# Nine closing operand splits of a two-block transformer kernel, moved on VectorE behind the weight split that followed them

## The reference, cut to what matters

```
u = rmsnorm(h, gain)          # h * rsqrt(mean(h*h)) * gain
h = h + mixer(u) @ w_out      # attention, gated delta rule, gated linear attention
u = rmsnorm(h, gain)
h = h + act(u @ w_up) @ w_down
```

## Time and profile before

| | us |
|---|---|
| median of 3 runs | 1652.29 |
| lowest, highest | 1652.26, 1653.44 |
| the profiled execution | 1653.44 |
| its span (first to last instruction) | 1651.6 |
| TensorE matmuls busy | 1575.7 (95%) |
| VectorE busy | 1119.3 (68%) |
| ScalarE busy | 792.4 (48%) |
| GpSimd busy | 185.2 (11%) |

### The profile page before, as it was taken

How to read it: one execution, slowest core, us unless ns; L and a number is a source line. 1 busy time by engine, 2 the same in 40 slices (tenths; PEclk the granted TensorE clock), 3 DMA queues, 4 the chain that set the end, 5 groups by cost and what they waited for, 6 DMA issues and landing times.

```text
span 1651.6 us, 31485 instructions
## 1 busy us (share of the span) xinstructions
PE 1575.7 (95%) x12628; PEld 1516.1 (92%) x12628; DVE 1119.3 (68%) x2014; ACT 792.4 (48%) x1360; POOL 185.2 (11%) x200
## 2 busy tenths in 40 slices
PE   6988899999998899999999899999989999999997
PEld 5875898999998699999899899999989899999997
DVE  5884654767775767777777766666677566666666
ACT  4537234533453454444655465544455556554443
POOL 2680411100012120000200012000020002010000
PEclk9998799999999999999999999999999999999999
DMA  6411001454454125455443343555534444254652
GB/s 217 154 52 52 1 1 52 154 190 167 169 188 150 65 103 187 170 203 175 165 165 118 143 155 103 180 178 204 174 139 173 153 154 166 90 190 168 205 179 77
DMA packets 125813, 236.55 MB, mean 143 GB/s; under 512 B 2615, under 2 KB 50026, under 8 KB 125690
## 3 DMA queue, kind: packets, MB, share of 16 engines
q1 hardware_dynamic: 124393, 230.29, 40.2%
q0 software_dynamic: 1296, 4.53, 0.9%
HBM read 233.76 MB, written 1.05 MB: 142 GB/s over the span
## 4 chain that ended last, share of the span: by engine, by line
PE 85%; DVE 9%; ACT 2%; issue 2%; DMA 1%; POOL 0%; SPq 0%; DVEq 0%; ACTq 0%; POOLq 0%
PE ps L613 48%; PE ps L660 6%; PE ps L659 6%; PE ps L658 6%; PE ps L621 5%; DVE w_lo L2212 3%; PE ps L803 2%; PE ps L764 1%; PE ps L987 1%; PE ps L709 1%; PE ps L969 1%; PE ps L744 1%; DVE mx L2558 1%; DVE hidden L2263 1%; ACT w_hi L1582 1%
## 5 line engine op out<-in xcount | busy, mean ns | idle before, releaser
L1582 ACT ACTIVATE w_hi<-raw 128x1024 fp32r<-128x1024 f32 x440 | 460.9, 1051 | 294.1 <-PE ps L660 137.9
L2212 DVE TENSOR_TENSOR w_lo<-raw,w_hi 128x1024 fp32r<-128x1024 f32 x440 | 544.8, 1239 | 8.1 <-ACT w_hi L1582 8.0
L613 PE MATMUL ps<-u_hi,w_hi 128*128 128x256 f32 (+1 forms) x1480 | 430.1, 291 | 11.9 <-DVE w_lo L2212 4.7
L613 PE MATMUL ps<-u_hi,w_lo 128*128 128x256 f32 (+1 forms) x1480 | 423.6, 286 | 0.0
L613 PE MATMUL ps<-u_lo,w_hi 128*128 128x256 f32 (+1 forms) x1480 | 423.2, 286 | 0.0
L613 PEld LDWEIGHTS ps<-u_hi,w_hi 128*128 128x128 f32 x1480 | 283.6, 192 | 17.3 <-issue 7.1
L613 PEld LDWEIGHTS ps<-u_hi,w_lo 128*128 128x128 f32 x1480 | 283.5, 192 | 0.0
L613 PEld LDWEIGHTS ps<-u_lo,w_hi 128*128 128x128 f32 x1480 | 282.6, 191 | 0.6
L613 PE MATMUL ps<-a_hi,w_hi 128*128 128x256 f32 (+1 forms) x864 | 246.4, 285 | 4.1 <-DVE a_lo L2232 2.0
L613 PE MATMUL ps<-a_lo,w_hi 128*128 128x256 f32 (+1 forms) x864 | 243.8, 282 | 0.0
L613 PE MATMUL ps<-a_hi,w_lo 128*128 128x256 f32 (+1 forms) x864 | 243.6, 282 | 0.0
(11 more groups left out here) (416 smaller groups left out, 2300.5 us busy)
## 6 DMA issues: line engine op xcount, KB each, us to landing
raw<-in_w_ff_dram SPq DMA_DIRECT2D x32, 2048.0 KB, 8.5
raw<-in_ffn_w_gu_dram SPq DMA_DIRECT2D x44, 1024.0 KB, 6.7
raw<-in_ffn_w_down_dram SPq DMA_DIRECT2D x10, 2048.0 KB, 7.9
raw<-in_xa_w_kv_dram SPq DMA_DIRECT2D x8, 2048.0 KB, 9.0
raw<-in_od_w_in_dram SPq DMA_DIRECT2D x6, 2048.0 KB, 8.1
raw<-in_w_in_ab_dram SPq DMA_DIRECT2D x5, 2048.0 KB, 7.9
raw<-in_ev_w_in_dram SPq DMA_DIRECT2D x5, 2048.0 KB, 7.9
raw<-in_xa_w_q_dram SPq DMA_DIRECT2D x4, 2048.0 KB, 7.8
```

The costliest lines, as they stand in the source:

```text
L613: mm = pe.matmul(bank[:, 0:n], wx[:, q, k * P:(k + 1) * P], x[ux][:, k, ts], start=k == 0 and i == 0, stop=k == KD - 1 and i == 2)
L1582: act.activation(quarter(w_hi, b, q), raw_quarter(b, q), ACT.Copy).then_inc(high_split, 1)
L2212: dve.tensor_tensor(quarter(w_lo, b, q), raw_quarter(b, q), quarter(w_hi, b, q).bitcast(F32), ALU.subtract)\
```

## The change

In `residual` and in `down`, the low part of the last chunk (k = 7) was issued right after that of chunk 6. It is now issued after the loop, that is behind the `split_low` of the next product's quarter 2, which came after it before. No instruction is added or removed, and only VectorE's queue changes.

```diff
@@ residual
                     if 4 * i + t >= 1:
                         finish_low(4 * i + t - 1, norm, ts)
-                    if 4 * i + t == KD - 1:
-                        finish_low(KD - 1, norm, ts)
                 stream(name, evac)
+                finish_low(KD - 1, norm, ts)
@@ down
                     if norm is not None and k >= 1:
                         finish_low(k - 1, norm, ts)
-                    if norm is not None and k == KD - 1:
-                        finish_low(k, norm, ts)
                     if k % 2 == 1:
                         split_low(b + 1, k // 2 - 1, g)
+                if norm is not None:
+                    finish_low(KD - 1, norm, ts)
```

## The result

| | before | after |
|---|---|---|
| median, us | 1652.55 (7 runs, 1651.36 to 1656.15) | 1671.59 (7 runs, 1659.86 to 1674.21) |
| ratio | | 1.0093, interval 1.0070 to 1.0115 |
| profiled execution: span, mean clock | 1651.6 us, 0.981 | 1661.9 us, 0.981 |

The change makes the kernel slower, as forecast, but by more than the range of the prediction held: its 1663.0 was the highest time allowed. The two profiled spans, which have the same mean clock, differ by 10.3 us; the medians of seven differ by 19.0. So there are two questions: what the move costs, and what stands between 10 and 19. An execution is one run of the whole kernel on the chip; executions of one and the same kernel differ here by 12 us and more.

What follows compares the result with a forecast made beforehand. The prediction took TensorE, 85% of the chain, as the bound. Its stalls, 3.80 + 0.66 + 3.42 + 0.8 = 8.7 us, on the median 1652.29 gave 1661.0, range 1656.0 to 1663.0.

Steps and rivals of the forecast that it cites:

- What moves, and who is late: At the nine seams: the split wins time, low 7 loses it, and TensorE waits for the later low 7.
- The earlier split: At the seams: writing quarter 2's weight split earlier is worth 0, being 2.9 us early already at c_out.
- the faster rival: TensorE waits for quarter 2 of the weights, so the earlier split pays 1.2 us nine times: 1641.5; chance 0.03.
- At a projection seam: Five seams of 256 tokens: TensorE stands 0.76 us for low 7 where it did not before, together 3.80 us.
- at ab_out: Seam ab_out to mlp0, 272 tokens: TensorE waits 0.66 us for the later low 7.
- At ev_in: Seam mlp1 to ev_in: TensorE already waits for low 7, which comes 1.71 us later in full.
- at od_in: Seam swiglu0 to od_in: same pattern as mlp1 to ev_in, 1.71 us again; together 3.42 us.
- at c_kv: Seam mlp0 to c_kv: the memory rows' load is issued later, costing 0.8 us; bounds 0.0 and 1.7.
- Low part ahead of the addition: At the seams: low 7 goes ahead of GpSimd's waiting addition; sum 5.1 us, 1657.4; chance 0.15.
- Full blocking behind a split: At eight seams: low 7 ends 0.48 us behind the addition, not 0.29; sum 10.2 us, 1662.5; chance 0.08.
- Stalls given back: Behind the seams: slack in later waits absorbs part of the 8.7 us, a third surviving; 1655.2 and less; chance 0.10.
- I count the stalls in full: Behind the seams: TensorE is the chain or waited on, so all stalls reach the end, 8.7 us slower.

Runs made afterwards that it cites:

- e8: The change plus 14 unread matmuls ahead of chunk 5 and 14 ahead of chunk 7 at od_in alone; stretch to od_in 195.35 us, whole 1.1 us below the change at one clock.
- e3: The whole change with GpSimd's eighth addition cut to one column; 4.4 us less than the change at one clock.
- e5: The change again, unchanged, beside new runs of the kernel before; 0.70% slower by the ratio, 11.6 us, and 8.1 us at one clock.
- e6: The kernel before against itself, nothing changed, side by side with e5; the kernel before showed 1651.4 to 1662.0 us in twelve executions there.

## Why the prediction was wrong

*What moves, and who is late.* Right. Low 7 ends 0.29 us behind the eighth addition at c_out, as rows 5 gave it, and starts TensorE 0.05 us later. The earlier split was worth nothing, and the faster rival (1641.5) didn't occur: no stretch but the one to mlp1 became shorter in both pairs, and there it is the shorter wait for the memory rows and the clock at 540 us, not quarter 2: TensorE has no wait for it at c_out.

*The terms.* At a projection seam 0.76 was forecast; 0.59 is measured between matmuls and 0.6 to 0.7 in the stretches. The step that is a little too large takes the start of chunk 7's weight load as the time at which its matmul would have run; the matmul comes 0.12 us later. For five seams that is some 3.3 in place of 3.80, at ab_out 0.52 for 0.66. At ev_in 1.67 for 1.71, at od_in 1.69 for 1.71 (e8), at c_kv 0.66 for 0.8. The waits sum to 7.8 us (3.3 + 0.52 + 3.36 + 0.66), forecast 8.7; at one clock the kernels differ by 8.9 (1664.5 - 1655.6). The 1.1 us between are not accounted for; e8, 1.1 below the change at one clock, suggests that a part of what the clock does at od_in is still in, but that is hardly more than the heights are known to.

*The rivals on the size.* Low part ahead of the addition: no, low 7 waits at every seam (0.96 us, and 0.48 in e3). Full blocking behind a split: no; low 7 would end 0.48 us behind the addition and ended 0.29. The rule of the Trainium skill ("SBUF — State Buffer", section "Who interferes with whom") has a loser wait out the winner's whole instruction; this trace agrees that GpSimd's instruction holds VectorE's up, but 0.19 us of the two records overlap (of which 0.08 is nothing special: low 6 and the split behind it overlap by as much, 612.71 + 0.48 against 613.11). Stalls given back: only at c_kv, which the sum held.

*The step that failed.* "I count the stalls in full. Sum ... 8.7 us slower", and the forecast then sets this sum on the median of three runs. The sum has no term for the granted clock. The clock came in twice. First, at od_in, where the sum has 1.71 us, the stretch grew by 3.8 to 4.0: the longer wait was followed by a piece at half clock. That is 2.1 to 2.4 us, and e8, with filler in both waits, doesn't have it. Second, the three runs of before, 1652.26 to 1653.44, were taken as the kernel's time, while 104 executions of it average 1656.9 at clock 0.979, and reach 1663. The change averages 1668.3 over 30. The difference of the averages is 11.4 us: 8.9 at one clock, and some 2.4 by the mean clock, which is 0.0022 lower (1.1 us for each 0.001). Those 2.4 us are nearly all od_in's piece, if it is in every execution as it is in both traces: 6.8 of some 1662 us at half clock lower the mean by 0.0020. The sum with od_in's 2.3 us in it would have been 11.0, close to the averages, but partly by luck: its waits are 0.9 us too large, and some 1.2 of the 11.4 us are not accounted for. What is between 11.4 and the 19.0 us of the first two medians may be the draw of seven executions each: five of the seven of the change had a clock of 0.971 to 0.976, and e5 and e6 did not show 19 again. But that isn't shown, and it isn't a likely draw: all seven of before were at or under 1656.2 us, as 54 of the other 104 are, a chance of about 1 in 100, so that those seven had something in common (a chip, an hour) can't be ruled out.

What stays open: why the clock between 140 and 200 us takes a better or a poorer course in an execution. It does so in both kernels, ahead of what was changed. The counts don't show that the change makes the poorer course more frequent: with od_in's 0.0020 allowed for, 15 of 30 executions of the change (clock 0.976 or less) stand against 43 of 104 of before (0.978 or less).

## What to carry to other kernels

A short instruction that the bottleneck engine waits for belongs ahead of a long one whose result is not due for microseconds; moved behind it, it pays for the long one, and for what another engine slips in between: here 0.11 and 0.48 us at a seam where TensorE had no wait before. When summing stalls on TensorE, look for other waits just ahead of each, and add what the next few microseconds cost at half clock, as a term with a chance: here 1.4 to 2.4 us behind six of nine long waits. And before setting a range, look at how far the windows of the kernel before are from full clock. This kernel has a stage with gaps and a clock of 0.7 to 0.8, and its executions spread over 12 us, though the first three agreed to 0.1%.

## What the runs showed of the hardware

- One kernel, always on one core, ran from 1651.3 to 1663.2 us in 104 executions, in step with its mean granted clock: 1.1 us for each 0.001. Of the 8.6 us between its two traces, 7.4 are made ahead of 313 us, where TensorE has gaps.
- In or behind a wait of 1.4 to 1.9 us TensorE's granted clock fell to half in six of nine unfilled cases, and 27 matmuls took 4.9 to 5.8 us and not 3.46: four of four where waits of 1.6 and 1.75 us had come just before, two of five where none had.
- Matmuls that nobody reads in the last of three such waits came too late (the clock fell while they ran, and 14 took 2.86 us and not 1.75); with 14 more in the wait before it, the clock stayed at 1.00 (one trace each).
- A GpSimd addition of one column took 0.64 us beside a VectorE split, one of 256 columns 1.18. Both records began 0.60 us before the split's end, and ended 0.04 and 0.58 us behind it: the first 0.60 is waiting.
